# Segment sums of the even mixer: fp32 products per head, or fp32r products of four heads at once

## The chip, the cores and the metric

The kernel runs on one core of one Trainium2 chip. The metric is the time of one execution on the device, in microseconds (us); before and after are medians of several executions. PE is TensorE, DVE is VectorE, ACT is ScalarE, POOL is GpSimd, SP is SyncE, which issues the loads. PEld is PE's loading of weights.

## What is computed

A decoder trunk of two layers over 256 tokens of width 1024, all in float32. Each layer has a SwiGLU, a mixer, a cross attention and a second SwiGLU. The change is in the first layer's mixer, whose Mamba-2 part has eight heads and works in two chunks of 128 tokens. What matters of it:

```python
cums = jnp.cumsum(dt * a, axis=2)                  # per chunk, over its 128 steps
seg = cums[:, :, :, None] - cums[:, :, None, :]    # sum of dt*a over steps s+1..l
lmat = jnp.exp(jnp.where(causal, seg, -jnp.inf))
cb = jnp.einsum('bclgn,bcsgn->bclsg', cc, bc)
y_diag = jnp.einsum('bclsg,bclsge,bcsgep->bclgep', cb, lmat, xdt)
```

`seg` is what the text calls the segment sums: for each head and chunk a 128x128 matrix.

## The kernel before

Weights come in chunks of 1 MB (128 partitions x 2048 float32) through a ring of three buffers. SP loads chunk n into `raw` once chunk n - 3 has been split. ACT writes its rounded high part `w_hi` (L701 in `hi_upto`) once PE has finished chunk n - 3. DVE writes the low part `w_lo`, raw minus high (L1241 in `lo_upto`), which this text calls the split. PE then multiplies in fp32r, three products for each pair (high by high, low by high, high by low: L1984, L1985, L1986; L2005 and L2012 in other projections), so that the result is nearly float32. fp32r is a 4-byte type that PE takes rounded, in one pass; plain float32 operands are also used, for small products.

The order on every engine is written out by hand in one function per engine (`even()` for the mixer), and engines wait for each other with semaphores. No planner sets it. In the even mixer the chunks are, in order, `x0 x1 x2 q0 q1 k0 k1 v0 v1 g0 g1 z0 z1`, and PE goes through them in that order:

- `x0` to `x2` give the convolution's input. DVE evacuates each (L1552) to `xpad`, ACT makes the fourth tap (L982), DVE adds three taps to each of two tiles (L1541 in `taps`, a group of six instructions per chunk, with a wait on itself after each pair), and ACT applies the Silu (L1063 in `conv_silu`). ACT does this inside a loop over c = 0, 1, 2, with the high parts of the coming chunks between, and after the third Silu writes the high parts of four more (`k1` and what follows, L701).
- In the turn c = 1, DVE makes `dt` and `dta` (= dt * a, 128 x 16: two chunks x eight heads) at L1567 and L1569, and signals `dta_done`.
- POOL's `even()` first calls `seg_weights` twice (L1943): for each chunk and head it multiplies the constant 128x128 triangle `after` with the column of `dta` of that head, into `ld`, which lies on `xk`. 16 instructions in all. After them it does its half of the rotation of queries and keys (L1921, L1922), four times in turn with DVE (L1526 in `rotate`, which waits for POOL's answer to the one before), then L1925 and the products L1929 and L1931.
- DVE's `even()` after the taps: the split of `k1`; then four times a rotation (L1526), each followed by a split. The masks `cbm` (L1580) stand before the fourth rotation. Then `xdt` (L1588).
- PE after `k1` transposes (L2356, L2360), makes four small products (L2366), and projects `v0` in two halves: the first needs rotation 1 to have read its bank, the second rotation 2. Then it makes two small products for the decays (L2373, L2374) and the segment sums (L2381): for each quarter q (a chunk and four heads) four float32 products of `ld` of one head with the triangle `upto`. ACT exponentiates each quarter (L1009) into `mt`, which lies on `xv`. Then `v1`, `g0` and so on.

PE's small fp32r products of the time steps (L2132) and the rows of L2119 come just before `x0`. In the FFN before the mixer ACT splits small tables between its turns (L1184, L1186), beside its usual L804, L811, L818 and L823.

```python
for q in range(4):
    pe.wait_ge(es["ld_done"], 4 * q + 4)
    if q == 2:
        pe.wait_ge(es["cbm_done"], 2)
    for h in range(4):
        last = mm(ps[:, 4 + q, h * P:(h + 1) * P], ev.ld[:, q // 2, 4 * (q % 2) + h, :],
                  const("upto"), start=True, stop=True)
    last.then_inc(es["seg_mm"], 1)
```

Of the kernel before, what the change touches and what calls it, by code (L numbers as in the profile page):

```python
# [20 lines left out]
F32 = mybir.dt.float32  # L21
F32R = mybir.dt.float32r
BF16 = mybir.dt.bfloat16
ALU = mybir.AluOpType
ACT = mybir.ActivationFunctionType
AX = mybir.AxisListType

P = 128
SEQ, MEM, D = 256, 256, 1024
TT = SEQ // P  # L30
# [12 lines left out]
SSM_H, HP, NS, SSM_IN = 8, 64, 64, 512  # L43
# [121 lines left out]
def build(nc, d, out):  # L165
# [3 lines left out]
    with ctx:  # L169
        def sb(name, shape, dt=F32):  # L170
            return ctx.enter_context(nc.sbuf_tensor(name, shape, dt))

        def LINES(n):

            return -(-n // 64) * 64
# [9 lines left out]
        def sem(name):  # L185
# [3 lines left out]
        ps = ctx.enter_context(nc.psum_tensor("ps", [P, 8, 512], F32))  # L189
# [21 lines left out]
        pT_parts = over("pT_parts", [P, 2, XH, 2, SEQ], placed() + 4 * 6144)  # L211
        arena = sb("arena", [P, LINES(ARENA)])
        small_parts = sb("small_parts", [P, LINES(2 * SMALL_W + 80)], F32R)
        small_w_hi, small_w_lo = ([small_parts[:, 2 * at_:2 * (at_ + KT * w)].rearrange("p (k i c) -> p k i c", i=2, c=w)[:, :, i, :]
                                   for at_, w in ((DT_AT, SSM_H), (GATE_AT, 3 * NH))] for i in range(2))
        small_w_k = [small_w[:, at_:at_ + KT * w].rearrange("p (k c) -> p k c", c=w)
# [223 lines left out]
        class Even:  # L440
            xpad = part(0, [XT, SEQ + 3])

            ld = xk[:, :, :].rearrange("p k c -> p (k c)").rearrange("p (t h s) -> p t h s", t=TT, h=SSM_H)
            xbcT = part(1920, [XT, SEQ])
            q_rot = part(3456, [TT, RET_H, 2, 64])
            o = part(3456, [TT, RET_H, P])
# [31 lines left out]
        ev = Even  # L478
# [206 lines left out]
        def _(act):  # L685
# [289 lines left out]
            def even():  # L975
                E = at["even", "x0"]
                row_copy(2, 7)
                for c in range(3):
                    act.wait_ge(es["xpad_done"], c + 1)
                    for m in range(2):  # L980
                        k = 2 * c + m
                        ins = nc.scalar.activation(ev.xbcT[:, k, :], ev.xpad[:, k, CONV_W - 1:], ACT.Identity,  # L982
                                                   bias=conv_b[:, k:k + 1], scale=conv_w[:, CONV_W - 1, k:k + 1])
                    ins.then_inc(es["act_read"], 1)
                    hi_upto(E + c + 4)
                    if c:
                        conv_silu(c - 1)
                    else:
                        act.wait_ge(es["dt_raw"], 1)
                        step(nc.scalar.activation(ev.ln1p, ev.dtr, ACT.Abs))  # L990
                        step(nc.scalar.activation(ev.ln1p, ev.ln1p, ACT.Exp, scale=-1.0))
                        nc.scalar.activation(ev.ea, head_rows[:, 1, :], ACT.Exp).then_inc(es["ea_done"], 1)
                        nc.scalar.activation(ev.ln1p, ev.ln1p, ACT.Ln, bias=1.0).then_inc(es["ln_done"], 1)
                conv_silu(2)
                for e in range(3, 7):
                    hi_upto(E + e + 4)

                for t in range(TT):
                    act.wait_ge(es["xs_T"], t + 1)
                    nc.scalar.activation(ev.xh[:, t, :, :], ps[:, 4 + t, :].rearrange("p (h c) -> p h c", h=SSM_H),  # L1000
                                         ACT.Copy).then_inc(es["xh_done"], 1)
                act.wait_ge(es["xs_T"], 3)
                nc.scalar.activation(ev.b_tok, ps[:, 0, 0:P], ACT.Copy).then_inc(es["xh_done"], 1)
                hi_upto(E + 7 + 4)
                act.wait_ge(es["dec_mm"], 1)
                nc.scalar.activation(ev.small[:, 72:88], ps[:, 0, P:P + 16], ACT.Exp).then_inc(es["dec_done"], 1)
                for q in range(4):
                    act.wait_ge(es["seg_mm"], q + 1)
                    nc.scalar.activation(ev.mt[:, q // 2, 4 * (q % 2):4 * (q % 2) + 4, :],  # L1009
                                         ps[:, 4 + q, :].rearrange("p (a c) -> p a c", a=4),  # L1010
                                         ACT.Exp).then_inc(es["seg_exp"], 1)
                act.wait_ge(chunks_used, E + 8 + 1)
                tokens_out(ev.v, (1, 2), ACT.Copy)
                for e in (8, 9):
                    hi_upto(E + e + 4)
                act.wait_ge(chunks_used, E + 10 + 1)
                tokens_out(xn[:, :, 0:512], (0, 3), ACT.Silu)
                hi_upto(E + 10 + 4)
                for i, dst in enumerate((ev.qT, ev.kT)):
                    for t in range(TT):  # L1020
                        act.wait_ge(es["qk_T"], 2 * i + t + 1)
                        nc.scalar.activation(dst[:, t, :, :], ps[:, 4 + 2 * i + t, :].rearrange("p (a c) -> p a c", a=4),
                                             ACT.Copy).then_inc(es["qkT_done"], 1)
                hi_upto(E + 11 + 4)
                act.wait_ge(chunks_used, E + 12 + 1)
                tokens_out(xn[:, :, 512:], (1, 2), ACT.Silu)
                hi_upto(E + 12 + 4)
                act.wait_ge(es["st_mm"], 1)
                nc.scalar.activation(ev.sT, ps[:, 6, :], ACT.Copy).then_inc(es["st_done"], 1)
                kv_chunk(0, 1)  # L1030
                act.wait_ge(es["ret_kv_mm"], 1)
                nc.scalar.activation(ev.kv, ps[:, 6, :].rearrange("p (a c) -> p a c", a=4),
                                     ACT.Copy).then_inc(es["kvs_done"], 1)
                kv_chunk(0, 2)
                for t in range(TT):

                    act.wait_ge(es["y_ready"], t + 1)
                    nc.scalar.activation(ev.xdt[:, t, :, :], ev.xh[:, t, :, :], ACT.Square,
                                         accum_out=ev.ssr[:, t:t + 1]).then_inc(es["y_sq"], 1)
                act.wait_ge(es["o_read"], 1)  # L1040
                act.wait_ge(es["y_read"], 1)
                nc.scalar.activation(ev.mt[:, :, 0:4, :], ev.o, ACT.Square).then_inc(es["o_sq"], 1)
                kv_chunk(0, 3)
                act.wait_ge(es["o_ssq"], 1)
                hi_upto(at["kv", 0, 4] + 4)
                act.wait_ge(chunks_used, at["kv", 0, 5] + 1)
                act.wait_ge(rstd_done, 4)
                for t, bank in enumerate((6, 5)):
                    nc.scalar.activation(xv[:, t, 0:2 * CW], ps[:, bank, :], ACT.Copy,
                                         scale=rstd_mem[:, t:t + 1]).then_inc(v_read, 1)  # L1050
                hi_upto(at["kv", 0, 5] + 4)
                evac_hi(SETS["mix0"], hT_hi)
                kv_chunk(0, 6)
# [7 lines left out]
            def conv_silu(c):  # L1061
                act.wait_ge(es["conv_done"], c + 1)
                nc.scalar.activation(ev.xbcT[:, 2 * c:2 * c + 2, :], ev.xbcT[:, 2 * c:2 * c + 2, :],  # L1063
                                     ACT.Silu).then_inc(es["xbc_done"], 1)
# [114 lines left out]
            def small_tables(c):  # L1179

                if c == 0:
                    act.wait_ge(small_in, SMALL)
                    for hi, src in zip(small_w_hi, small_w_k):
                        nc.scalar.activation(hi, src, ACT.Copy)  # L1184
                elif c == 1:
                    nc.scalar.activation(masks[:, :], masks_f, ACT.Copy).then_inc(consts_made, 1)  # L1186

            act.wait_ge(neg_half_set, 1)
# [667 lines left out]
        def _(pool):  # L1856
# [55 lines left out]
            def even():  # L1912
                pool.wait_ge(x_added, 4)
                G.memset(ev.xpad[:, :, 0:CONV_W - 1], 0.0).then_inc(es["xpad_zero"], 1)
                seg_weights(0)
                seg_weights(1)
                for i in range(4):
                    pool.wait_ge(es["rot_read"], i + 1)
                    a, b, c, e = ev.rot
# [16 lines left out]
                pool.wait_ge(es["o_ssq"], 1)  # L1936
                inv_rms(ev.ors, ev.oms, ev.osq, 8, DK).then_inc(es["o_rstd"], 1)

            def seg_weights(t):

                pool.wait_ge(es["dta_done"], 1)
                for h in range(SSM_H):
                    G.tensor_scalar(ev.ld[:, t, h, :], const("after"),  # L1943
                                    ev.dta[:, 8 * t + h:8 * t + h + 1], None, ALU.mult).then_inc(es["ld_done"], 1)

            G.memset(neg_half[:, :], -0.5).then_inc(neg_half_set, 1)
            pool.wait_ge(neg_half_set, 1)
# [31 lines left out]
        def _(pe):  # L1979
# [336 lines left out]
            def even():  # L2316
# [57 lines left out]
                mm(ps[:, 0, P + 8:P + 16], const("upto"), ev.dta[:, 8:16], start=True, stop=True)\  # L2374
                    .then_inc(es["dec_mm"], 1)
                for q in range(4):
                    pe.wait_ge(es["ld_done"], 4 * q + 4)
                    if q == 2:
                        pe.wait_ge(es["cbm_done"], 2)
                    for h in range(4):  # L2380
                        last = mm(ps[:, 4 + q, h * P:(h + 1) * P], ev.ld[:, q // 2, 4 * (q % 2) + h, :],  # L2381
                                  const("upto"), start=True, stop=True)
                    last.then_inc(es["seg_mm"], 1)
                project_half(8, 1, (1, 2))
                project_half(9, 0, (0, 3), (("dec_done", 1), ("rot_read", 4)))
# [356 lines left out]
```

## Time and profile before

| | us |
|---|---|
| median of 3 executions | 1206.31 |
| lowest, highest | 1204.7, 1207.48 |
| the profiled execution's own time | 1206.05 |
| its span in the trace | 1204.1 |
| PE busy | 1193.1 (99% of the span) |
| DVE busy | 794.2 (66%) |
| ACT busy | 642.3 (53%) |
| POOL busy | 119.8 (10%) |

The mean granted clock of PE over the span is 0.997 of full speed. The profiled execution takes 1.95 us more than its span: what lies before the first and after the last instruction. Busy time of PE is the union of its matmuls, whose ends are modelled: a matmul with 512 columns stands with 0.39 us, but the next one starts 0.23 us after it. So the rate of PE is read from starts, not from durations. Also on DVE and ACT the next instruction may start some 0.08 us before the one ahead of it ends.

### The profile page before, as it was taken

How to read it: one execution, taken by the hardware profiler on the slowest of the kernel's cores; microseconds unless marked ns; L12 is line 12 of the kernel's file. 1: busy time of each engine (PE TensorE's matmuls, PEld its weight loads, DVE VectorE, ACT ScalarE, POOL GpSimd, SP SyncE). 2: the span in 40 equal slices, each digit the busy share in tenths (PEclk: the TensorE clock that was granted, in tenths of full speed). 3: DMA queues.
4: the chain of work that ended last, by engine and by line, in shares of the span. 5: the costliest groups of instructions: out<-in, count | busy, mean ns of one | idle time of the engine just before them, and what ended most of it. 6: DMA issues, size and time to landing. Idle time of an engine off the chain costs nothing.

```text
span 1204.1 us, 17654 instructions
## 1 busy us (share of the span) xinstructions
PE 1193.1 (99%) x6995; PEld 1047.3 (87%) x6995; DVE 794.2 (66%) x841; ACT 642.3 (53%) x871; POOL 119.8 (10%) x105
## 2 busy tenths in 40 slices
PE   9999999999999999999999999999999999999997
PEld 8888889889989888888888888899978898888886
DVE  6766766865757676566676665667785676666664
ACT  7545546553556554444564544454666565544443
POOL 1010001630132010000020000020002121000001
PEclk9999999999999999999999999999999999999999
DMA  9966654554444466565556555655632435656560
GB/s 319 342 198 193 192 187 163 175 157 144 139 155 141 140 214 203 178 204 179 174 177 207 187 196 178 204 167 154 206 123 88 133 113 167 235 185 198 178 206 35
DMA packets 164880, 214.75 MB, mean 178 GB/s; under 512 B 14816, under 2 KB 140896, under 8 KB 164704
## 3 DMA queue, kind: packets, MB, share of 16 engines
q1 hardware_dynamic: 164544, 213.30, 54.9%
q8 instruction: 33, 0.54, 0.2%
q0 software_dynamic: 144, 0.52, 0.1%
q10 hardware_dynamic: 144, 0.26, 0.1%
q14 instruction: 15, 0.12, 0.0%
HBM read 213.02 MB, written 1.05 MB: 178 GB/s over the span
## 4 chain that ended last, share of the span: by engine, by line
PE 96%; ACT 1%; DVE 1%; DMA 0%; issue 0%; POOL 0%; POOLq 0%; DVEq 0%
PE ps L2005 30%; PE ps L2012 16%; PE ps L1984 15%; PE ps L1985 15%; PE ps L1986 15%; PE ps L2069 1%; ACT xn L1173 1%; PE ps L2524 0%; PE ps L2613 0%; PE ps L2674 0%; PE ps L2651 0%; DMA arena<-in_first 0%; PE ps L2280 0%; PE ps L2132 0%; PE ps L2381 0%
## 5 line engine op out<-in xcount | busy, mean ns | idle before, releaser
L2005 PE MATMUL ps<-hT,w_hi 128*128 128x512 f32 x1568 | 374.9, 391 | 0.9 <-ACT w_hi L750 0.7
L2005 PEld LDWEIGHTS ps<-hT,w_hi 128*128 128x128 f32 x1568 | 290.1, 188 | 58.9 <-DVE hT L1281 1.0
L1396 DVE TENSOR_TENSOR w_lo<-raw,w_hi 128x2048 fp32r<-128x2048 f32 x108 | 247.6, 2293 | 61.8 <-ACT w_hi L831 61.8
L1241 DVE TENSOR_TENSOR w_lo<-raw,w_hi 128x2048 fp32r<-128x2048 f32 x85 | 195.2, 2306 | 72.5 <-ACT w_hi L701 72.5
L701 ACT ACTIVATE w_hi<-raw 128x2048 fp32r<-128x2048 f32 x85 | 162.1, 1913 | 87.4 <-PE ps L1986 85.8
L2012 PEld LDWEIGHTS ps<-hT,w_lo 128*128 128x128 f32 x1568 | 201.6, 191 | 8.0
L831 ACT ACTIVATE w_hi<-raw 128x2048 fp32r<-128x2048 f32 x108 | 205.9, 1906 | 0.8 <-DMA raw<-in_ffn_w_gate 0.8
L2012 PE MATMUL ps<-hT,w_lo 128*128 128x256 f32 x1568 | 204.0, 283 | 0.0
L1984 PE MATMUL ps<-w_hi,arena_r 128*128 128x512 f32 x354 | 138.5, 391 | 0.0
L1985 PE MATMUL ps<-w_lo,arena_r 128*128 128x512 f32 x354 | 137.9, 389 | 0.0
L1986 PE MATMUL ps<-w_hi,arena_r 128*128 128x512 f32 x354 | 137.5, 388 | 0.0
L1874 POOL TENSOR_SCALAR msq<-msum 128x1 f32<-128x1 f32 x18 | 27.8, 1545 | 664.5 <-ACT xn L711 582.0
L1984 PE MATMUL ps<-w_hi,hT 128*128 128x512 f32 (+1 forms) x240 | 91.6, 381 | 0.0
L804 ACT ACTIVATE arena<-ps 128x512 f32<-128x512 f32 x44 | 26.4, 599 | 122.0 <-PE ps L2012 122.0
L1985 PE MATMUL ps<-w_lo,hT 128*128 128x512 f32 (+1 forms) x240 | 90.2, 376 | 0.0
L1986 PE MATMUL ps<-w_hi,hT 128*128 128x512 f32 (+1 forms) x240 | 90.2, 376 | 0.0
L823 ACT ACTIVATE arena_r<-arena 128x512 fp32r<-128x512 f32 x44 | 27.8, 631 | 112.3 <-PE ps L1986 105.7
L818 ACT ACTIVATE arena<-ps 128x512 f32<-128x512 f32 x44 | 26.3, 597 | 106.6 <-PE ps L2012 106.6
L1986 PEld LDWEIGHTS ps<-w_hi,arena_r 128*128 128x128 f32 x354 | 66.5, 188 | 14.0
L1984 PEld LDWEIGHTS ps<-w_hi,arena_r 128*128 128x128 f32 x354 | 66.7, 188 | 12.6 <-issue 0.2
L1985 PEld LDWEIGHTS ps<-w_lo,arena_r 128*128 128x128 f32 x354 | 66.7, 188 | 12.0
L1377 DVE TENSOR_TENSOR arena<-arena,ps 128x512 f32<-128x512 f32 x44 | 30.3, 688 | 57.2 <-ACT arena L818 57.2
(320 smaller groups left out, 1632.1 us busy)
## 6 DMA issues: line engine op xcount, KB each, us to landing
raw<-in_ffn_w_down SPq DMA_DIRECT2D x44, 1024.0 KB, 4.9
raw<-in_ffn_w_gate SPq DMA_DIRECT2D x43, 1024.0 KB, 5.3
raw<-in_ffn_w_up SPq DMA_DIRECT2D x43, 1024.0 KB, 5.3
raw<-in_xattn_wkv SPq DMA_DIRECT2D x16, 1024.0 KB, 5.4
raw<-in_even_w_in SPq DMA_DIRECT2D x13, 1024.0 KB, 5.1
raw<-in_xattn_wq SPq DMA_DIRECT2D x8, 1024.0 KB, 5.1
raw<-in_xattn_wo SPq DMA_DIRECT2D x8, 1024.0 KB, 4.9
raw<-in_odd_w_in SPq DMA_DIRECT2D x6, 1024.0 KB, 5.6
```

The source lines that it names most:

```text
L701: ins = nc.scalar.activation(hi, src, ACT.Copy)
L823: nc.scalar.activation(dst, gu.rearrange("p (k c) -> p k c", k=2), ACT.Copy).then_inc(gu_hi_done, 1)
L831: nc.scalar.activation(w_hi[:, m % RING, :], raw[:, m % RING, :], ACT.Copy).then_inc(hi_done, 1)
L1241: ins = V.tensor_tensor(lo, src, hi.bitcast(F32), ALU.subtract)
L1377: V.tensor_tensor(up, up_lo, ps[:, 2:4, 0:SEQ], ALU.add).then_inc(up_read, 1)
L1396: V.tensor_tensor(w_lo[:, m % RING, :], raw[:, m % RING, :], w_hi[:, m % RING, :].bitcast(F32), ALU.subtract).then_inc(lo_done, 1)
L1874: step(G.tensor_scalar(msq[:, t:t + 1], msum[:, sum_at(v, t):sum_at(v, t) + 1], msum[:, sum_at(v, t) + 1:sum_at(v, t) + 2], EPS, ALU.add, ...
L1984: mm(dst, l_hi, r_hi, start=start, stop=False)
L1985: mm(dst, l_hi, r_lo, start=False, stop=False)
L1986: return mm(dst, l_lo, r_hi, start=False, stop=stop)
L2005: mm(ps[:, bank0 + m, :], cols(w_hi, n, k, CW, m * P, (m + 1) * P), hT[:, k, :, :].rearrange("p a c -> p (a c)"), start=k == 0, stop=False)
L2012: last = mm(ps[:, bank0 + m, SEQ:], cols(w_lo, n, k, CW, m * P, (m + 1) * P), hT[:, k, 0, :], start=False, stop=k == KT - 1)
```

## The change

The sum over steps s+1..l can be written as a product of `after` with `upto` times `dta` as well as of `after` times `dta` with `upto`. The changed kernel scales `upto` instead, which is the moving operand, so four heads (512 columns) fit one product, and `after` is the same weight for all. To run in fp32r, `dta` is divided into a high part (rounded by ACT) and a low part (the rest, POOL); `after` and `upto` hold only 0 and 1. Each quarter is then two products of 512 columns, added up in PSUM.

- ACT copies `after` to an fp32r tile `after_r` in the FFN before (beside L1186), and writes the high part of `dta` after the Silu at c = 1, once `dta_done` is 1.
- POOL waits for `dta_done` 2, subtracts the high part (128 x 16) with a wait on itself, and makes eight tensor_tensor instructions of 128x512 (four quarters, high and low), `upto` repeated over four heads times the column of each head repeated over 128, to fp32r. They go to `xk_parts` and `xv_parts`, which lie on `xk` and `xv`.
- PE waits per quarter for `ld_done` q + 1 and makes two fp32r products in place of four float32 ones.

```diff
@@ even: tiles
+        dta_parts = small_parts[:, 2 * SMALL_W + 80:2 * SMALL_W + 112].rearrange("p (i c) -> p i c", i=2)
+        after_r = sb("after_r", [P, P], F32R)
...
-            ld = xk[:, :, :].rearrange("p k c -> p (k c)").rearrange("p (t h s) -> p t h s", t=TT, h=SSM_H)
+            upto_hi = xk_parts[:, :, :].rearrange("p k c -> p (k c)").rearrange("p (t h s) -> p t h s", t=TT, h=SSM_H)
+            upto_lo = xv_parts[:, :, :].rearrange("p t (h s) -> p t h s", h=SSM_H)
@@ scalar engine, even() and small_tables()
                     if c:
                         conv_silu(c - 1)
+                        if c == 1:
+                            act.wait_ge(es["dta_done"], 1)
+                            nc.scalar.activation(dta_parts[:, 0, :], ev.dta, ACT.Copy).then_inc(es["dta_done"], 1)
...
                 elif c == 1:
+                    nc.scalar.activation(after_r[:, :], const("after"), ACT.Copy)
                     nc.scalar.activation(masks[:, :], masks_f, ACT.Copy).then_inc(consts_made, 1)
@@ gpsimd
-                seg_weights(0)
-                seg_weights(1)
+                seg_weights()
...
-            def seg_weights(t):
-
-                pool.wait_ge(es["dta_done"], 1)
-                for h in range(SSM_H):
-                    G.tensor_scalar(ev.ld[:, t, h, :], const("after"),
-                                    ev.dta[:, 8 * t + h:8 * t + h + 1], None, ALU.mult).then_inc(es["ld_done"], 1)
+            def seg_weights():
+
+                pool.wait_ge(es["dta_done"], 2)
+                dta_hi, dta_lo = (dta_parts[:, i, :].bitcast(F32) for i in range(2))
+                step(G.tensor_tensor(dta_parts[:, 1, :], ev.dta, dta_hi, ALU.subtract))
+                upto = const("upto").unsqueeze(1).to_broadcast([P, 4, P])
+                for q in range(4):
+                    for dst, src in ((ev.upto_hi, dta_hi), (ev.upto_lo, dta_lo)):
+                        ins = G.tensor_tensor(dst[:, q // 2, 4 * (q % 2):4 * (q % 2) + 4, :], upto,
+                                              src[:, 4 * q:4 * q + 4].unsqueeze(2).to_broadcast([P, 4, P]), ALU.mult)
+                    ins.then_inc(es["ld_done"], 1)
@@ tensor engine, even()
                 for q in range(4):
-                    pe.wait_ge(es["ld_done"], 4 * q + 4)
+                    pe.wait_ge(es["ld_done"], q + 1)
                     if q == 2:
                         pe.wait_ge(es["cbm_done"], 2)
-                    for h in range(4):
-                        last = mm(ps[:, 4 + q, h * P:(h + 1) * P], ev.ld[:, q // 2, 4 * (q % 2) + h, :],
-                                  const("upto"), start=True, stop=True)
+                    for i, part_ in enumerate((ev.upto_hi, ev.upto_lo)):
+                        last = mm(ps[:, 4 + q, :], after_r[:, :],
+                                  part_[:, q // 2, 4 * (q % 2):4 * (q % 2) + 4, :].rearrange("p h s -> p (h s)"),
+                                  start=i == 0, stop=i == 1)
                     last.then_inc(es["seg_mm"], 1)
```

## Rows read from the trace of the kernel before

**Rows 1.** The page: busy time by engine, and the chain that ended last.

```profile
PE 1193.1 (99%) x6995; PEld 1047.3 (87%) x6995; DVE 794.2 (66%) x841; ACT 642.3 (53%) x871; POOL 119.8 (10%) x105
...
PE 96%; ACT 1%; DVE 1%; DMA 0%; issue 0%; POOL 0%; POOLq 0%; DVEq 0%
```

**Rows 2.** PE's timeline: start us, us, engine, line, operation, tiles, form, count.

```profile
234.59 0.39 PE L1984 MATMUL ps<-w_hi,hT 128*128 128x512 f32 x1
...
244.63 0.50 PE L1984 MATMUL ps<-w_hi,hT 128*128 128x512 f32 x1
...
247.89 3.82 PE L2381 MATMUL ps<-consts,xk 128*128 128x128 f32 x32
251.46 0.48 PE L1984 MATMUL ps<-w_hi,hT 128*128 128x512 f32 x1
```

**Rows 3.** Waits from 215 to 262 us: total us, times, longest.

```profile
DVE arena L1526 <- POOL arena L1922: 3.5, 3, 1.4
...
PEld ps L1984 <- DVE arena L1526: 0.3, 1, 0.3
```

**Rows 4.** DVE's timeline over the taps and rotations, and all 18 taps.

```profile
213.29 2.71 DVE L1541 SCALAR_TENSOR_TENSOR arena<-arena,conv_w 128x256 f32<-128x256 f32 x6
...
219.44 2.88 DVE L1541 SCALAR_TENSOR_TENSOR arena<-arena,conv_w 128x256 f32<-128x256 f32 x6
222.49 2.29 DVE L1241 TENSOR_TENSOR w_lo<-raw,w_hi 128x2048 fp32r<-128x2048 f32 x1 [0.18 <-ACT w_hi L701]
224.70 3.00 DVE L1541 SCALAR_TENSOR_TENSOR arena<-arena,conv_w 128x256 f32<-128x256 f32 x6
230.21 2.29 DVE L1241 TENSOR_TENSOR w_lo<-raw,w_hi 128x2048 fp32r<-128x2048 f32 x1 [2.51 <-ACT w_hi L701]
...
242.92 1.66 DVE L1526 SCALAR_TENSOR_TENSOR arena<-ps,rstd,consts 128x256 f32<-128x256 f32 x4 [1.39 <-POOL arena L1922]
...
L1541 DVE SCALAR_TENSOR_TENSOR arena<-arena,conv_w x18: 471/484/594, 213.3 to 227.2; 128x256 f32<-128x256 f32 x18
```

**Rows 5.** ACT's timeline, in the FFN before and around the taps.

```profile
167.63 0.63 ACT L823 ACTIVATE arena_r<-arena 128x512 fp32r<-128x512 f32 x1 [2.34 <-PE ps L1986]
...
209.38 0.20 ACT L990 ACTIVATE arena<-arena 128x16 f32<-128x16 f32 x1
...
219.56 1.09 ACT L982 ACTIVATE arena<-arena,conv_b,conv_w 128x256 f32<-128x256 f32 x2 [1.31 <-DVE arena L1552]
...
227.73 0.63 ACT L1063 ACTIVATE arena<-arena 128x512 f32<-128x512 f32 x1 [4.75 <-DVE arena L1541]
228.27 3.70 ACT L701 ACTIVATE w_hi<-raw 128x2048 fp32r<-128x2048 f32 x2
```

**Rows 6.** POOL's timeline: the 16 instructions of seg_weights.

```profile
219.02 14.53 POOL L1943 TENSOR_SCALAR xk<-consts,arena 128x128 f32<-128x128 f32 x16 [20.26 <-DVE arena L1569]
```

**Rows 7.** DVE and POOL beside each other; L1895 and L1377 by their lines.

```profile
251.38 1.04 POOL L1925 TENSOR_TENSOR arena<-arena,consts 128x512 f32<-128x512 f32 x1
...
251.41 2.10 DVE L1588 TENSOR_TENSOR arena<-arena 128x1024 f32<-128x1024 f32 x1 [1.59 <-POOL arena L1922]
253.43 2.28 DVE L1241 TENSOR_TENSOR w_lo<-raw,w_hi 128x2048 fp32r<-128x2048 f32 x1
...
253.59 3.03 POOL L1929 TENSOR_TENSOR arena<-arena,head_rows 128x512 f32<-128x512 f32 x1 [1.16 <-DVE arena L1588]
...
L1895 POOL TENSOR_TENSOR xv_parts<-xv,xn_parts x8: 1282/1516/3422, 371.8 to 976.2; 128x512 fp32r<-128x512 f32 x8
...
L1377 DVE TENSOR_TENSOR arena<-arena,ps 128x512 f32<-128x512 f32 x44 | 30.3, 688 | 57.2 <-ACT arena L818 57.2
```

**Rows 8.** PE's timeline before the mixer: fp32r products of 512 columns.

```profile
197.50 2.02 PE L2132 MATMUL ps<-hT,small_parts 128*128 128x512 f32 x8
199.36 0.61 PE L2119 MATMUL ps<-consts,rstd 128*128 128x128 f32 x4
```

**Rows 9.** The page: loads, KB each, median us from issue to landing.

```profile
raw<-in_even_w_in SPq DMA_DIRECT2D x13, 1024.0 KB, 5.1
```

## The prediction

> **What bounds the kernel now.** I read the page's busy shares and its chain first [rows 1]: PE is busy 99% of a span of 1204.1 us, and 96% of the chain that ended last is PE. So time goes only where PE's own stream gets shorter, or where PE is made to wait. The profiled execution took 1206.05 us, 0.26 us below the median of 1206.31; a difference worked out on it carries over to the median unchanged. About 0.2%, 2.4 us, is what a measurement of this kernel can tell from no change.
>
> Then PE's timeline around the edit [rows 2]. The segment sums are 32 records (each of the 16 products is two) from 247.89 us; the next project begins at 251.46. They cost 3.57 us of PE.
>
> Then PE's waits in this stretch, and DVE and ACT in order of time [rows 3, 4, 5]. PE looks covered, but one row matters: PE's weight load of L1984 waited 0.3 us for DVE L1526, the rotation. It is the second half of chunk `v0` (L1984 at 244.63 [rows 2]), which waits for the third rotation (242.92 + 1.66 = 244.58). So the rotations arrive with no slack at all, although PE is never long idle. I followed them back. It had waited 1.39 us for POOL's answer to rotation 1, that one for the answer to rotation 0, and rotation 0 stands on DVE right behind the split of `k1` (L1241 at 230.21). That split waited for ACT's w_hi at 228.27, which stands in ACT's queue behind the last Silu at 227.73, which had waited 4.8 us for the taps on DVE (L1541) that ended at 227.70. From the second and third group of taps to PE at 244.63 there is one serial chain, DVE, ACT, DVE, POOL, DVE, PE, whose slack is zero. A delay of the taps is a delay of PE.
>
> **What POOL does beside those taps.** POOL's 16 old instructions run from 219.02 to 233.55 [rows 6], over the same stretch as taps 2 and 3. In the first group of taps, before POOL starts, six take 2.71 us; the next two groups take 2.88 and 3.00 [rows 4]. So the old work already costs the chain 0.17 + 0.29 = 0.46 us. POOL's other instructions show how the two engines hold each other up [rows 7]. DVE L1588 (128x1024) takes 2.10 us beside POOL's 128x512 L1925, which began 0.03 us earlier; between the 512 and the 2048 wide DVE forms (L1377 0.69, L1241 2.29 us) such an instruction is worth 1.22, so it stood still for 0.88 us of POOL's 1.04. And the other way round, POOL's L1929 takes 3.03 us and ends 0.90 us after DVE's w_lo (253.43 + 2.28 = 255.71), where L1925, as large, takes 1.04. In each case both engines read two SBUF operands, and one waits for the other. POOL's old 128-wide tensor_scalar held DVE much less: single taps are 0.59 us at worst against a median of 0.48 [rows 4].
>
> The Trainium skill (SBUF — State Buffer, "Who interferes with whom") says that a DVE instruction with two SBUF inputs and a GpSimd instruction that reads SBUF exclude each other, for the whole instruction. The rows agree on the exclusion. On "whole" they differ: 0.88 of 1.04 us, and about 0.11 of 0.60 for the tensor_scalar. By the page's wording eight new instructions would hold DVE 8 x 1.04 = 8.3 us, and the total would come to some 1211.9.
>
> **The change, part by part.**
> - PE: 32 records are replaced by 8 fp32r products of 512 columns. The nearest row is L2132, eight fp32r products of 512 columns from 197.50, followed by L2119 at 199.36: 1.86 us [rows 8]. Gain 3.57 - 1.86 = 1.71 us. The bounds are near: at the rate of the old records, 0.112 us for 128 columns, with each column passed once instead of twice, 512 columns are 0.223 us and the gain is 1.79; with a record's whole 0.39 us for each, it is 0.45. I take the row that is alike. All of it is on PE. The switch of number kind (L1984 at 251.46 takes 0.48 us instead of the usual 0.39) only moves to the front of the group.
> - ACT, one copy of 128x16 after the Silu at c = 1. It waits for `dta`, which released POOL at 219.02 [rows 6], and takes 0.20 us like L990 of the same size [rows 5]. What is behind it, L982, began at 219.56, having waited 1.31 us for DVE: the copy ends at about 219.2 and costs nothing; without that cover it would cost its 0.2 us. The copy of `after` in the FFN is 128x128, between the 0.20 of L990 and the 0.63 us of L823 (128x512), in the 2.34 us for which ACT waits for PE at 167.63. Nothing; uncovered it would be that much.
> - POOL: it starts at 219.27 instead of 219.02. The subtraction of 16 columns with its step is an estimate, 0.3 us, half of what L1943 takes for 128. Then eight tensor_tensor of 128x512 with a broadcast operand. L1925, of that kind, takes 1.04; L1895, two dense operands to fp32r, 1.28 at least, and 3.42 behind a DVE split. I take 1.04, since one operand is a broadcast as in L1925. Alone that is 8.3 us instead of 14.5; with DVE's turns in between, the last ends at about 231.5, ahead of the rotations, whose first will end at some 240. PE needs the first quarter at 247.9: no wait for `ld_done`.
> - DVE, which the diff doesn't touch, pays. Each POOL instruction starts right after the one before and holds DVE for 0.88 of its 1.04 us, so it asks again about 0.16 us after it has let go, while a tap runs 0.4 (0.48 less its overlap with the next); so they take turns, tap, POOL, tap, POOL. All eight fit in before taps 3 end. Without POOL the stretch from 219.44 is 2.71 + 2.21 (the split, less its overlap of 0.08) + 2.71 = 7.63, to 227.07. Add 8 x 0.88 = 7.04, less about 0.4 us for the pauses between taps that POOL now fills (an estimate: 2.71 us is six times 0.4 and 0.3 over): 233.7 instead of 227.70, 6.0 us late.
> - The rest of that chain. Silu, w_hi and split follow unchanged (227.70 to 232.50, 4.8 us), done at 238.5. PE wants `k1` at 234.59 [rows 2]: first stall, 3.9 us. Rotation 2 ends at 244.58 + 6.0 = 250.6, PE would be there at 244.63 + 3.9: second stall, 2.1 us. Together 6.0. The masks for `cbm_done` are made on DVE behind rotation 2 and a split and move by the same 6.0, as PE does: no new wait. DMA: `g0` is loaded once `k1` is split, at 238.5, lands in 5.1 us [rows 9] at 243.6, and ACT wants it when PE is done with `k1`, at 238.5 + 24 x 0.23 = 244.0. Covered by 0.4 us; if not, ACT is late there by what is missing.
>
> Sum: + 6.0 - 1.7 = **+ 4.3 us**, so 1210.6 by the median.
>
> **Rivals.**
> - *POOL holds DVE as little as its old instructions did.* For it: the old rows (0.11 us a tap). If the eight cost 8 x 0.11 = 0.9, in place of 0.46, the chain is 0.4 late: 1206.31 + 0.4 - 1.7 = 1205.0; with no hold at all, which also removes the old 0.46, 1204.1. Deciding point: below 1.7 us of added delay the change gains, below 4.1 it can't be told from none. Against it: the rows with 512-wide POOL work, all holding. Chance 0.22. This is the way to the other side.
> - *DVE keeps its turn through each pair of taps* (they are issued without a wait in a pair). For it: eleven old POOL instructions made two groups of taps only 0.46 us longer, so not every tap was held. Then one POOL instruction falls behind each of five pairs and one behind the split, six in all: 6 x 0.88 = 5.3 on 227.07, less the 0.63 that is already in 227.70, 4.6 late: 1209.2. Chance 0.22.
> - *Dense price on POOL.* At 1.28 us an instruction the hold is some 1.12: 9.0 instead of 7.0, 1212.6. For it: new results are fp32r, as with L1895. Against: the row with a broadcast. Chance 0.12.
> - *The change doesn't shorten PE*: eight products at 0.446 us each, 3.57 us as before; with the delay 1212.3. Against it: L2132's eight in 1.86. Chance 0.02.
> - My forecast: 0.42.
>
> **How the numbers follow.** 1210.6 is the likeliest. Eight in ten: from inside the first rival (1204.1 to 1205.0) to the dense price: 1204.4 to 1212.7. The likeliest case's own range, with 0.1 us more or less to a hold, is 1209.8 to 1211.4. Slower by over 2.4 us: forecast, dense price, the rival without the PE gain, and half of the pairs case, which is at + 2.9: 0.42 + 0.12 + 0.02 + 0.11 = 0.67. Faster by over 2.4 us is beyond the 2.2 that the best case can give, so noise alone: 0.06. The same: 0.27.
>
> **What would show it.** PE's group: eight products in about 1.86 us. DVE L1541: groups of six at some 6 to 7 us instead of 2.88, single taps of 1.2 to 1.4. POOL's new line: eight instructions, mean 1.2 us or more. ACT's third Silu near 233.7. Two idle stretches on PE, before L1984 near 234.6 (3.9 us, for the split) and before the second half of `v0` (2.1 us, for L1526). The prediction is wrong if the taps stay near 3 us, or if the third Silu is late and PE still has no gap.

## The result, and the profile after

The changed kernel takes 1210.03 us (median of 9 executions, 1208.42 to 1210.77), the kernel before 1206.21 us in the same comparison. The ratio is 1.0031, with a 95% interval of 1.0022 to 1.0040: slower by some 3.8 us. Forecast were 1210.6 us and + 4.3. The profiled execution took 1210.03 us, with a span of 1208.2, 4.1 above the span before.

The page after, busy time and chain:

```profile
PE 1193.5 (99%) x6971; PEld 1045.8 (87%) x6971; DVE 799.7 (66%) x841; ACT 643.0 (53%) x873; POOL 114.7 (9%) x98
...
PE 93%; DVE 3%; ACT 2%; POOL 1%; issue 1%; DMA 0%; POOLq 0%; DVEq 0%; ACTq 0%
```

PE is still busy for 99%, and POOL has less to do than before (114.7 us against 119.8). The busy shares of [rows 1] don't show the loss; of the chain, PE has 93% now instead of 96%. The timelines show where. DVE's, with its three groups of taps (L1548 now, L1541 before), the splits (L1248) and the third rotation (L1533):

```profile
213.40 2.70 DVE L1548 SCALAR_TENSOR_TENSOR arena<-arena,conv_w 128x256 f32<-128x256 f32 x6
...
219.56 6.38 DVE L1548 SCALAR_TENSOR_TENSOR arena<-arena,conv_w 128x256 f32<-128x256 f32 x6
225.86 3.12 DVE L1248 TENSOR_TENSOR w_lo<-raw,w_hi 128x2048 fp32r<-128x2048 f32 x1
228.91 4.27 DVE L1548 SCALAR_TENSOR_TENSOR arena<-arena,conv_w 128x256 f32<-128x256 f32 x6
235.68 2.29 DVE L1248 TENSOR_TENSOR w_lo<-raw,w_hi 128x2048 fp32r<-128x2048 f32 x1 [2.50 <-ACT w_hi L704]
...
248.41 1.66 DVE L1533 SCALAR_TENSOR_TENSOR arena<-ps,rstd,consts 128x256 f32<-128x256 f32 x4 [1.41 <-POOL arena L1928]
```

The first group is as it was. The second takes 6.38 us instead of 2.88, the split behind it 3.12 instead of 2.29, the third group 4.27 instead of 3.00 [rows 4]. Beside them stand POOL's new instructions, from its timeline and by their line:

```profile
219.37 0.22 POOL L1949 TENSOR_TENSOR small_parts<-arena,small_parts 128x16 fp32r<-128x16 f32 x1 [20.48 <-ACT small_parts L993]
219.67 1.26 POOL L1953 TENSOR_TENSOR xk_parts<-consts,small_parts 128x512 fp32r<-128x512 f32 x1
220.90 1.22 POOL L1953 TENSOR_TENSOR xv_parts<-consts,small_parts 128x512 fp32r<-128x512 f32 x1
...
226.80 3.08 POOL L1953 TENSOR_TENSOR xk_parts<-consts,small_parts 128x512 fp32r<-128x512 f32 x1
229.85 1.22 POOL L1953 TENSOR_TENSOR xv_parts<-consts,small_parts 128x512 fp32r<-128x512 f32 x1
```

Each starts some 1.2 us after the one before, one tap to one POOL instruction, until the split takes its turn and POOL waits 3.08 us. The eighth ends at 231.06. ACT's timeline carries the delay on, and PE's receives it:

```profile
219.07 0.22 ACT L993 ACTIVATE small_parts<-arena 128x16 fp32r<-128x16 f32 x1 [0.71 <-DVE arena L1576]
...
233.21 0.63 ACT L1069 ACTIVATE arena<-arena 128x512 f32<-128x512 f32 x1 [6.61 <-DVE arena L1548]
```

```profile
234.50 0.39 PE L1997 MATMUL ps<-w_hi,hT 128*128 128x512 f32 x1
238.03 0.79 PE L1995 MATMUL ps<-w_hi,hT 128*128 128x512 f32 x1 [3.15 <-DVE w_lo L1248]
238.62 0.63 PE L1996 MATMUL ps<-w_lo,hT 128*128 128x512 f32 x1
...
249.38 0.39 PE L1997 MATMUL ps<-w_hi,hT 128*128 128x512 f32 x1
250.12 0.50 PE L1995 MATMUL ps<-w_hi,hT 128*128 128x512 f32 x1 [0.36 <-DVE arena L1533]
...
253.38 0.49 PE L2392 MATMUL ps<-xk_parts,after_r 128*128 128x512 f32 x1
...
255.10 0.39 PE L2392 MATMUL ps<-xv_parts,after_r 128*128 128x512 f32 x1
```

The third Silu comes at 233.21 instead of 227.73. PE stands still before `k1`, from 234.73, where the next start was due, to 238.03, and again for 0.5 us before the second half of `v0`. The segment sums do what they should: from 253.38 PE needs 1.94 us to the next project's start at 255.32, against 3.57 in [rows 2].

PE after that first stop, in windows (span, busy us and count of PE, PEld, DVE, ACT, POOL, granted clock, share and rate of the DMAs):

```profile
234.50:238.00 3.50, 0.38 (x2) 0.00 (x0) 2.32 (x2) 3.50 (x3) 0.00 (x0) 0.95 0.00 0
238.00:240.80 2.80, 2.77 (x7) 2.19 (x8) 2.80 (x5) 1.25 (x1) 1.17 (x1) 0.50 0.59 148
240.80:245.00 4.20, 4.20 (x19) 3.43 (x18) 2.80 (x6) 0.00 (x0) 2.35 (x3) 0.97 0.90 297
```

Behind the stop PE is granted 0.50, the 1.2 GHz level, and its products start 0.43 us apart instead of 0.23, for some 3 us, until 2.4 GHz come back. The first seven products take 3.11 us; behind the same stop in `e1_pool_alone` (below), at 2.4 GHz, they take 1.72. The 1.4 us between them are lost, but not here: PE would only have waited longer for rotation 2, which ends at 250.07.

### The profile page after: what moved, and what is told of

Its sections match the earlier page's. It is cut to its first block, busy times and chain, and to the rows that moved or that the text cites. A ratio compares the mean times of both kernels' runs of the same rounds, so it can differ in the third digit from the quotient of the medians.

```text
span 1208.2 us, 17601 instructions
## 1 busy us (share of the span) xinstructions
PE 1193.5 (99%) x6971; PEld 1045.8 (87%) x6971; DVE 799.7 (66%) x841; ACT 643.0 (53%) x873; POOL 114.7 (9%) x98
## 4 chain that ended last, share of the span: by engine, by line
PE 93%; DVE 3%; ACT 2%; POOL 1%; issue 1%; DMA 0%; POOLq 0%; DVEq 0%; ACTq 0%
PE ps L2016 30%; PE ps L2023 16%; PE ps L1995 14%; PE ps L1996 14%; PE ps L1997 14%; PE ps L2080 1%; DVE arena L1548 1%; ACT xn L1179 1%; DVE w_lo L1248 1%; PE ps L2625 1%; PE ps L2536 0%; POOL arena L1927 0%; DVE arena L1533 0%; PE ps L2686 0%; DMA arena<-in_first 0%
## 5 line engine op out<-in xcount | busy, mean ns | idle before, releaser
L1248 DVE TENSOR_TENSOR w_lo<-raw,w_hi 128x2048 fp32r<-128x2048 f32 x85 | 196.1, 2316 | 71.1 <-ACT w_hi L704 71.0
```

The lines of the kernel that those rows point to most:

```text
L1248: ins = V.tensor_tensor(lo, src, hi.bitcast(F32), ALU.subtract)
```

## The experiments

Theory A is the prediction's: POOL's wide two-operand instructions hold DVE's taps, a serial chain carries this to PE, and PE's own part is a gain. Theory B: PE's new form, or the new waits, cost the time. The executions scatter by steps of some 1.5 us (more on it in the last section), so beside the ratio I give, from each trace, the time from the start of the second group of taps to PE's transposes of the rotated queries, which follow `g1`:

| kernel | us | against before |
|---|---|---|
| before | 267.89 - 219.44 = 48.45 | |
| changed | 271.66 - 219.56 = 52.10 | + 3.65 |
| e1_pe_alone | 267.54 - 220.85 = 46.69 | - 1.76 |
| e1_pool_alone | 273.14 - 219.38 = 53.76 | + 5.31 |
| e1_four_wide | 272.97 - 220.96 = 52.01 | + 3.56 |
| e1_on_act | 267.57 - 221.02 = 46.55 | - 1.90 |
| e2_write_only | 266.02 - 219.48 = 46.54 | - 1.91 |
| e2_one_operand | 270.20 - 219.68 = 50.52 | + 2.07 |
| e2_narrow | 275.54 - 219.53 = 56.01 | + 7.56 |
| e2_after_taps | 269.99 - 219.48 = 50.51 | + 2.06 |
| e3_old_sums_on_act | 267.98 - 219.72 = 48.26 | - 0.19 |
| e3_on_act_again | 266.12 - 219.59 = 46.53 | - 1.92 |

The rows of `e1_four_wide` and `e2_one_operand` hold 1.6 us each of time lost to products at 1.2 GHz, as their sections show; in the changed kernel and `e2_narrow` the wait for rotation 2 takes such products in. The table has one execution of each kernel.

### The two halves of the change

`e1_pe_alone`: the new products, the old kind of work on POOL. `e1_pool_alone`: the new work on POOL and ACT, the old kind of products. Both against the changed kernel:

```diff
@@ e1_pe_alone
+                pool.wait_ge(es["dta_done"], 1)
+                for q in range(4):
+                    for h in range(4):
+                        col = 4 * q + h
+                        ins = G.tensor_scalar(ev.upto_hi[:, q // 2, 4 * (q % 2) + h, :], const("upto"),
+                                              ev.dta[:, col:col + 1], None, ALU.mult)
+                    ins.then_inc(es["ld_done"], 1)
...
-                    for i, part_ in enumerate((ev.upto_hi, ev.upto_lo)):
+                    for i, part_ in enumerate((ev.upto_hi, ev.upto_hi)):
@@ e1_pool_alone
-                    for i, part_ in enumerate((ev.upto_hi, ev.upto_lo)):
-                        last = mm(ps[:, 4 + q, :], after_r[:, :],
...
+                    for h in range(4):
+                        last = mm(ps[:, 4 + q, h * P:(h + 1) * P], const("after"),
+                                  ev.upto_hi[:, q // 2, 4 * (q % 2) + h, :].bitcast(F32), start=True, stop=True)
```

> PE's part alone: POOL makes 16 narrow tensor_scalar of upto times dta as before the change, ACT makes no high part, and PE makes the eight fp32r products. The low part is left out: the high tile stands in for it, so every sum comes out twice. Theory A (the time goes to POOL's wide instructions holding the taps on DVE, PE's part is a gain): groups of taps 2.88 and 3.00 us as before, no idle stretch of PE near 234.6, the eight products in 1.94 us to the next start, time 1206.2 - 1.7 = 1204.5. Theory B (PE's new form is what costs, by the fp32r products or the switch into them): 1208 or more.

> POOL's and ACT's part as in the changed kernel, but PE makes 16 float32 products of 128 columns again, triangle after as the weight and the high part as the moving operand. The low part is made but left out of the sums. Theory A: the second group of taps 6.4 us and the third 4.3, third Silu at 233.2, PE idle 3.3 us before the project of k1, and now nothing given back: 1210.0 + 1.7 = 1211.7. Theory B: taps don't matter to the end, time 1206.2.

Measured: `e1_pe_alone` 1204.6 us against 1206.0, ratio 0.9990 (0.9981 to 0.9999). `e1_pool_alone` 1211.27 against 1206.0, ratio 1.0038 (1.0025 to 1.0052). From the timelines of DVE and PE, first of PE's half; then of DVE and ACT for POOL's half, with its waits:

```profile
220.85 2.88 DVE L1545 SCALAR_TENSOR_TENSOR arena<-arena,conv_w 128x256 f32<-128x256 f32 x6
...
249.25 2.11 PE L2387 MATMUL ps<-xk_parts,after_r 128*128 128x512 f32 x8
251.20 0.40 PE L1990 MATMUL ps<-w_hi,hT 128*128 128x512 f32 x1
```

```profile
219.38 6.38 DVE L1548 SCALAR_TENSOR_TENSOR arena<-arena,conv_w 128x256 f32<-128x256 f32 x6
...
233.03 0.63 ACT L1069 ACTIVATE arena<-arena 128x512 f32<-128x512 f32 x1 [6.61 <-DVE arena L1548]
...
PE ps L1995 <- DVE w_lo L1248: 3.2, 1, 3.2
...
PE ps L1995 <- DVE arena L1533: 1.8, 1, 1.8
```

Both are as theory A had them. The halves add up: - 1.76 + 5.31 = + 3.55, against + 3.65 for the whole. Theory B is out: PE's new form alone is a gain. `e1_pool_alone` had no slow clock after its first stop (24 starts at full rate), and by the waits its second stop was 1.8 us instead of 0.4. So the clock after the stop and the second stop stand in for each other.

### Four wide instructions instead of eight

The kernel before, with float32 results and nothing else of the change:

```diff
-                seg_weights(0)
-                seg_weights(1)
+                seg_weights()
...
+            def seg_weights():
+                pool.wait_ge(es["dta_done"], 1)
+                after = const("after").unsqueeze(1).to_broadcast([P, 4, P])
+                for q in range(4):
+                    G.tensor_tensor(ev.ld[:, q // 2, 4 * (q % 2):4 * (q % 2) + 4, :], after,
+                                    ev.dta[:, 4 * q:4 * q + 4].unsqueeze(2).to_broadcast([P, 4, P]),
+                                    ALU.mult).then_inc(es["ld_done"], 4)
```

> The kernel before, with POOL's 16 narrow tensor_scalar replaced by four wide tensor_tensor (128x512, float32) that write the same ld; PE, ACT as before. Theory A: the delay goes by the number of wide instructions. Eight made the stretch of the taps 13.6 us instead of 7.6 without POOL, 0.75 each; four make it 3.0 longer, against 0.6 longer in the kernel before: 2.4 us late, 1208.6; first delayed group of taps 5.8 us. Rival (what delays is the fp32r output, the new tiles or the added waits): 1206.2 or a little less, since POOL works only 5 us instead of 14.5.

Measured: 1207.94 us against 1206.0, ratio 1.0013 (1.0004 to 1.0022). POOL now works 4.6 us in this stretch instead of 14.5, and the kernel is slower. DVE's and PE's timelines, and PE's window behind the stop:

```profile
220.96 5.41 DVE L1541 SCALAR_TENSOR_TENSOR arena<-arena,conv_w 128x256 f32<-128x256 f32 x6
226.28 2.28 DVE L1241 TENSOR_TENSOR w_lo<-raw,w_hi 128x2048 fp32r<-128x2048 f32 x1
228.48 2.71 DVE L1541 SCALAR_TENSOR_TENSOR arena<-arena,conv_w 128x256 f32<-128x256 f32 x6
...
248.12 0.50 PE L1985 MATMUL ps<-w_hi,hT 128*128 128x512 f32 x1 [1.76 <-DVE arena L1526]
...
248.10:251.10 3.00, 2.98 (x9) 2.34 (x10) 2.83 (x3) 0.00 (x0) 2.95 (x2) 0.64 0.45 174
```

Four holds: 5.41 - 2.71 = 2.70, 0.68 each. The taps end 10.23 us after the second group began, against 8.26 before: 1.97 late (2.4 expected), which is the measured + 1.9. The type of the result, the new tiles and the new waits are not needed for the delay. The profiled execution, 1211.15, is the slowest of its eleven: here the slow clock came behind the stop for rotation 2, where no later wait takes it in, and its 1.6 us are in the table's + 3.56.

### What POOL must do to hold DVE

Three edits of POOL's eight instructions: a write without a read, one operand instead of two, and four narrow ones for each wide one.

```diff
@@ e2_write_only
+                        ins = G.memset(dst[:, q // 2, 4 * (q % 2):4 * (q % 2) + 4, :].bitcast(F32), -0.01)
@@ e2_one_operand
+                        ins = G.tensor_scalar(dst[:, q // 2, 4 * (q % 2):4 * (q % 2) + 4, :], upto,
+                                              src[:, 4 * q:4 * q + 1], None, ALU.mult)
@@ e2_narrow
+                        for h in range(4):
+                            ins = G.tensor_scalar(dst[:, q // 2, 4 * (q % 2) + h, :], const("upto"),
+                                                  src[:, 4 * q + h:4 * q + h + 1], None, ALU.mult)
```

> The changed kernel with each of POOL's eight wide tensor_tensor replaced by a memset of the same tile with -0.01; dta is left out of the sums, PE does the same eight products. If it is POOL's reads that hold the taps: groups of taps 2.7 us both, third Silu no later than 4.8 us after the second group began plus 3 (as in the run with the copies on ACT, 8.0 us), no idle stretch of PE, and a time like that run, some 2 below before. If any POOL instruction on these tiles, or its writing, holds them: the first group at 4 us or more.

> The changed kernel with the eight tensor_tensor as tensor_scalar of the same 128x512: one tensor operand read instead of two. Left out: all four heads of a quarter get the first head's factor. If the hold goes by what POOL reads: a 128 wide tensor_scalar held a tap for about 0.11 us, so this one holds for some 0.43 us, half of the wide tensor_tensor; both groups of taps and the split together some 3 us longer than without POOL instead of 5.9; time some 1206.7. If it goes by the instruction's whole duration (some 0.9 us): nearly as late as the changed kernel, 1209.

> The changed kernel with the eight wide tensor_tensor as 32 tensor_scalar of 128x128, nothing left out. Theory A: the taps are nearly free (groups 2.9 and 3.0 us, third Silu as in the kernel before, no idle stretch of PE before the project of k1), but POOL is not done in time: 16 took 14.5 us, 32 take 24 or more, to about 244, so its answer to rotation 0 comes some 9 us late and PE stands still before the halves of v0. Time 1206 + 9 - 1.7, some 1213 to 1214. If lateness on POOL's own queue didn't matter: 1204.5.

Measured, one execution each, against 1204.81 us for before: 1204.89, 1209.05 and 1214.02. The executions of before lie between 1204.19 and 1207.67 here, so one time says little, and the table and the rows decide. The time of `e2_write_only` isn't 2 us below before, as expected; its row of the table is (- 1.91). DVE and POOL in `e2_write_only`:

```profile
219.48 2.70 DVE L1548 SCALAR_TENSOR_TENSOR arena<-arena,conv_w 128x256 f32<-128x256 f32 x6
...
219.57 0.53 POOL L1952 MEMSET xk_parts<- 128x512 f32 x1
220.04 0.53 POOL L1952 MEMSET xv_parts<- 128x512 f32 x1
```

Eight memsets from 219.57 to 223.38 hold nothing: the taps take 2.70 us. The Trainium skill (SBUF — State Buffer, "Who interferes with whom") says of a GpSimd instruction that only writes that it doesn't contend with DVE; this trace agrees. In `e2_one_operand`:

```profile
219.68 3.38 DVE L1548 SCALAR_TENSOR_TENSOR arena<-arena,conv_w 128x256 f32<-128x256 f32 x6
...
240.18 1.66 DVE L1533 SCALAR_TENSOR_TENSOR arena<-ps,rstd,consts 128x256 f32<-128x256 f32 x4 [2.85 <-POOL arena L1928]
...
226.68 1.77 POOL L1953 TENSOR_SCALAR xv_parts<-consts,small_parts 128x512 fp32r<-128x512 f32 x1
...
234.97 3.71 POOL L1953 TENSOR_SCALAR xv_parts<-consts,small_parts 128x512 fp32r<-128x512 f32 x1
```

A held tap takes 0.91 instead of 0.48 us: the hold is 0.43, as expected. The sum was missed all the same (1206.7 expected, + 2.07 in the table instead of + 0.7). I had taken 0.9 us for this instruction; it takes 1.57 to 1.77, only a quarter of which it holds DVE. So the taps end just 0.8 us late, but POOL isn't done before 238.7, and its answer to rotation 0 makes DVE wait 2.85 us instead of 1.40. Rotation 2 is 2.3 us late by both, which less PE's 1.76 is + 0.5: near the + 0.7, but by another road than expected, so by luck. The other 1.6 us of the + 2.07 are PE's clock behind its stop for rotation 2, where again no later wait takes them in:

```profile
247.10:250.50 3.40, 3.36 (x8) 2.68 (x9) 2.85 (x3) 0.00 (x0) 3.33 (x2) 0.50 0.51 167
```

By element that POOL reads in a partition the holds are alike: 0.11 us for the 128 of a narrow tensor_scalar, 0.43 for 512, 0.78 for the two operands of 512 in the changed kernel, that is 0.86, 0.84 and 0.76 ns. This speaks for the reads; but the last two differ in the kind of instruction too, and no run parts the two.

`e2_narrow` shows the second road alone:

```profile
219.53 2.82 DVE L1548 SCALAR_TENSOR_TENSOR arena<-arena,conv_w 128x256 f32<-128x256 f32 x6
...
247.05 1.66 DVE L1533 SCALAR_TENSOR_TENSOR arena<-ps,rstd,consts 128x256 f32<-128x256 f32 x4 [10.68 <-POOL arena L1928]
...
DVE arena L1533 <- POOL arena L1928: 12.8, 3, 10.7
```

Taps nearly as before, and a rotation 9.3 us late (247.05 against 237.67, where the taps began 0.09 us earlier). + 7.56, that is 9.3 less PE's 1.76, as expected.

### The same work after the taps

```diff
                 pool.wait_ge(es["dta_done"], 2)
+                pool.wait_ge(es["conv_done"], 3)
```

> The changed kernel with POOL waiting also for the last taps (conv_done 3) before its eight wide instructions; nothing left out. Theory A: taps 2.7 us a group, third Silu 0.5 us earlier than before the change; the split of k1 is now held for 0.9 us, and POOL, working for 8.3 us plus the split's 2.2 from where the taps end, is late for rotation 0 by some 3.5 us. PE then waits for the rotation: 1206.1 + 3.3 - 1.7 = 1207.7, between before and the changed kernel. Rival (only the sum of POOL's and DVE's work in the stretch counts, wherever it stands): 1210 as the changed kernel.

Measured: 1208.53 us against 1204.81, ratio 1.0027 (1.0018 to 1.0037); + 2.06 in the table.

```profile
224.74 2.71 DVE L1548 SCALAR_TENSOR_TENSOR arena<-arena,conv_w 128x256 f32<-128x256 f32 x6
229.96 3.13 DVE L1248 TENSOR_TENSOR w_lo<-raw,w_hi 128x2048 fp32r<-128x2048 f32 x1 [2.50 <-ACT w_hi L704]
...
241.51 1.66 DVE L1533 SCALAR_TENSOR_TENSOR arena<-ps,rstd,consts 128x256 f32<-128x256 f32 x4 [4.38 <-POOL arena L1928]
```

By the trace the place of the work matters: this kernel is 1.6 us better than the changed one. The expected 3.3 us for PE's waits came out as 3.8 (2.06 + 1.76), since two splits, not one, stood in POOL's way. The times don't show the 1.6 us: the median is 3.72 us above before, that of the changed kernel 3.82, and the interval here is 2.2 to 4.5 us. One reason may be the clock. The profiled execution kept 2.4 GHz behind its stop of 2.3 us for rotation 2:

```profile
248.40:251.80 3.40, 3.33 (x17) 2.81 (x18) 2.88 (x4) 0.20 (x1) 3.31 (x2) 1.00 0.48 170
```

Behind stops of 1.9 and 2.3 us `e1_four_wide` and `e2_one_operand` paid 1.6 us; 2.06 + 1.6 would be the 3.7 of the median. That the other executions paid it is not shown. So the rival, for which only the sum of the work counts, is out by the trace, not by the times. Between the end of the taps and the answer to rotation 0 POOL has 6.4 us free (227.45 to 233.90 in `e2_write_only`), less than the 8.3 us of this work. Spreading the eight over the pauses between rotations was not tried.

### The work on ACT

POOL keeps the small subtraction and signals it; ACT makes both tiles in three of its waits:

```diff
+                scaled = [(q, i, 4 * q + h) for q in range(4) for i in range(2) for h in range(4)]
+
+                def scale_upto(n):
+                    for q, i, col in scaled[:n]:
+                        dst = (ev.upto_hi, ev.upto_lo)[i]
+                        ins = nc.scalar.activation(dst[:, col // 8, col % 8, :], const("upto"), ACT.Copy,
+                                                   scale=dta_parts[:, i, col:col + 1].bitcast(F32))
+                        if i and col % 4 == 3:
+                            ins.then_inc(es["ld_done"], 1)
+                    del scaled[:n]
+
+                act.wait_ge(es["dta_done"], 3)
+                scale_upto(12)
                 conv_silu(2)
                 for e in range(3, 7):
                     hi_upto(E + e + 4)
+                    if e in (4, 5):
+                        scale_upto(8 if e == 4 else 12)
```

> The changed kernel with POOL's eight wide instructions gone: ACT makes the same two tiles in 32 copies of 128x128 with a scale per partition, 12 in its wait for the third group of taps, 8 and 12 in its next two waits for PE; POOL keeps the subtraction of 16 columns. Nothing is left out. Theory A: taps 2.7 us each, third Silu near 227.2 to 227.7, no idle stretch of PE, time 1206.2 - 1.7 = 1204.5, at best 0.1 lower. Rival (any work added between dta and the sums delays the chain, here through ACT's own queue: 12 copies of 0.29 are 3.4 us in a wait of 4.8): 1206 or more.

> The kernel before (float32 sums, 16 products), with POOL's 16 narrow tensor_scalar gone: ACT makes the same ld in 16 copies of 128x128, 12 in its wait for the third group of taps, 4 after the high part of v0. Nothing is left out. It parts the gain of the run with the copies on ACT (1203.93 against 1206.0): if PE's shorter stream is all of it, this one is like the kernel before, 0.1 us lower at most (PE's small wait for rotation 2), though the third Silu comes some 0.3 us earlier. If taking POOL away from the taps gains by itself: 1205.6 or less.

> The run with fp32r sums and the copies on ACT once more, beside the one above on the same chip: 1.7 to 2.1 us below the kernel before, and 1.6 to 1.8 below the run above.

Measured: `e1_on_act` 1203.93 us against 1206.0, ratio 0.9977 (0.9968 to 0.9986). Once more: 1204.04 against 1206.02, ratio 0.9983 (0.9974 to 0.9992). The old sums with ACT's work: 1205.6 against 1206.02, ratio 1.0000 (0.9991 to 1.0009). The repetition lies 1.56 us below that one by the medians (1.6 to 1.8 expected) and 1.73 by the table. ACT and DVE in the first:

```profile
226.29 2.71 DVE L1563 SCALAR_TENSOR_TENSOR arena<-arena,conv_w 128x256 f32<-128x256 f32 x6
...
226.81 1.27 ACT L1005 ACTIVATE xk_parts<-consts,small_parts 128x128 fp32r<-128x128 f32 x4
229.03 0.63 ACT L1084 ACTIVATE arena<-arena 128x512 f32<-128x512 f32 x1 [0.95 <-DVE arena L1563]
```

Twelve copies fit in front of the third Silu, which still waits 0.95 us. PE waits for no engine in this stretch. This is the version that is faster than both: 2.0 us below before, 6 below the changed kernel. The old sums with ACT's copies give - 0.19 in the table. Their median is just the 1205.6 that I had set for a gain without PE's part, but the ratio of 1.0000 doesn't bear a gain out, and the median moves with how many executions fall on each step of the scatter. So PE's shorter stream is nearly all of the gain, and taking POOL away from the taps is worth little while nothing else waits.

## Why the prediction was right

- **PE's gain.** Forecast 1.71 us. In the changed kernel the eight products and the switch before them take 255.56 - 253.38 = 2.18 us to the start of the next project's second product, against 3.89 before (251.78 - 247.89): 1.71. Alone it measured 1.76.
- **ACT.** The copy ended at 219.29, 0.39 us before L985, which waited for DVE. Nothing, as forecast.
- **DVE's taps.** Forecast 6.0 us late; the stretch from the second group is 13.62 us (to 233.18) instead of 8.26: 5.4 late. Two errors stood against each other. Without POOL the stretch isn't 7.63 but 7.97 us (`e2_write_only`, 219.48 to 227.45), because the split then waits 0.35 us for ACT's high part. And the hold is less than 0.88 us: 0.78 where a tap has no pause before it (1.26 - 0.48), and (13.62 - 7.97) / 8 = 0.71 of delay for each instruction, since part of the holds falls into pauses. By the wording of the Trainium skill (SBUF — State Buffer, "Who interferes with whom") it would be the whole 1.04 us that the instruction takes alone; the trace has less. They take turns one by one, as forecast: POOL's period of 1.18 us is a hold of 0.78 and a tap of 0.40.
- **The chain to PE.** Silu, high part and split took 4.8 us as forecast (233.18 to 237.98). The first stop was 3.3 us (3.9 forecast), the second 0.5 (2.1). The sum of both is 2.2 smaller than forecast. 0.6 of it is the taps, and 1.4 the clock, which I hadn't thought of: the slow products lie where the second stop was to be. The last 0.2 are small: PE came to `k1` 0.14 us later than before, and the first product behind a stop takes 0.1 longer. That the clock costs nothing here is luck; in `e1_four_wide` and `e2_one_operand` it does. The total is set by rotation 2: 250.07 - 244.58 = 5.5 less the 0.12 by which this execution's taps began later, 5.4.
- **Sum.** + 5.4 - 1.7 = + 3.7, measured + 3.8. The 0.5 by which + 4.3 was too high is the taps, the two errors of opposite sign.
- **Rivals.** "Holds as little as its old instructions" is out for wide ones and true for narrow ones (`e2_narrow`, groups of 2.82 and 3.00 us). "DVE keeps its turn through a pair" is out: second taps of a pair take 1.26 us. "Dense price" is out: POOL's 1.22 us for its instructions is the turn-taking, 1.04 without it (`e2_after_taps`). The rival with no gain on PE is out.

## What to carry to other kernels

Where PE is busy for 99%, look at the waits that are just met: a row of 0.3 us of PEld waiting for DVE marked a chain with no slack, and what held an engine on it cost full price (taps 1.97 us late, time + 1.9). When POOL's work is regrouped into fewer, wider instructions, count for how long it holds DVE and for how long it keeps its own queue, not its sum: 16 narrow instructions (14.5 us) cost this kernel less than four wide ones (4.6 us). Small elementwise work that would run beside DVE can go into ACT's waits, if they are there: here that made 6 us of difference.

## What was not expected of the hardware

A tensor_scalar on POOL over 128x512 with a broadcast operand takes 1.57 to 1.77 us where no split stands in its way, against 1.04 for a tensor_tensor of that size, yet holds DVE for only 0.43.

PE's clock after a short stop is not the same in each execution. Behind the stop of 3.3 us at 234.7 the changed kernel was granted 1.2 GHz for some 3 us, `e1_pool_alone`, with as long a stop, was not. A stop that every profiled execution has, of 1.87 us near 880, shows both: behind it nine of the twelve were granted 1.2 GHz, the three with the work on ACT were not. Whether that is more than chance is not shown. The window of 3.9 us behind it, first in the kernel before, then in the repetition of the work on ACT:

```profile
882.10:886.00 3.90, 3.88 (x21) 3.27 (x22) 3.13 (x6) 0.20 (x1) 0.00 (x0) 0.58 0.71 269
```

```profile
880.40:884.30 3.90, 3.90 (x35) 3.59 (x36) 3.83 (x7) 1.02 (x6) 0.00 (x0) 1.00 0.76 269
```

21 products against 35 in the same time. From the transposes at which the table ends to PE's end the first takes 929.93 us, the second 928.37: 1.56 us.

A second such place is behind PE's wait at 5.1 us (1.2 us in the kernel before and in `e1_on_act`). Three of the profiles (`e1_pe_alone`, `e1_four_wide`, `e1_on_act`) have 9 starts of products from 7 to 10 us, the others 16 or 17. The granted clock stands as 1.00 there in all of them, so that it is the clock is read from the starts alone. `e1_on_act` and its repetition are the same kernel, both at full clock behind the stop near 880. The first has 9 starts, the second 16; its second group of taps begins at 221.02 against 219.59, 1.43 us later, and it took 1204.06 us against 1202.58.

Two places that each cost 1.5 us or nothing fit the three levels at which the 28 executions of the kernel before in one comparison stand: 1204.3 to 1204.9, 1205.9 to 1206.4 and 1207.4 to 1207.9. The profile of before, with slow products near 880 and none at the start, took 1206.05, the middle level. That all the levels come from these two places is argued from twelve profiles, not shown. What decides it in an execution stays open.
